# Gated projections and the last up projection with the weights as the stationary operand

## What is computed

```python
def swiglu(h, w_gu, w_down):                       # layers a and b, D_FF = 2816
    gate, up = jnp.split(h @ w_gu, 2, axis=-1)
    return (jax.nn.silu(gate) * up) @ w_down

x = x + swiglu(rmsnorm(x, norm_ffn), w_gu, w_down)            # layers a and b
h = rmsnorm_2(x, norm_mlp[l])                                 # last layer, D_FF_2 = 4096
x = x + jnp.square(jax.nn.relu(h @ w_mlp_in[l])) @ w_mlp_out[l]
```

## Time and profile before

| | us |
|---|---|
| median of 3 runs (lowest, highest) | 972.89 (972.74, 973.11) |
| the profiled execution | 973.31 |
| its span | 971.5 |
| PE busy | 961.4 (99%) |
| LDWEIGHTS busy | 779.4 (80%) |
| DVE busy | 576.1 (59%) |
| ACT busy | 497.2 (51%) |
| DMA | 168.79 MB, mean 174 GB/s |

### The profile page before, as it was taken

One profiled execution on the slowest core, in us unless ns is written; L12 is line 12 of the kernel. 1 busy time (PEld: TensorE's weight loads), 2 busy tenths in 40 slices (PEclk: granted clock), 3 DMA queues, 4 the chain that ended last, 5 costly groups with the idle time before them and its releaser, 6 DMA issues.

```text
span 971.5 us, 12509 instructions
## 1 busy us (share of the span) xinstructions
PE 961.4 (99%) x4848; PEld 779.4 (80%) x4848; DVE 576.1 (59%) x846; ACT 497.2 (51%) x694; POOL 5.7 (1%) x13
## 2 busy tenths in 40 slices
PE   9999999999999999999999999999999999999996
PEld 7878888888888887888888888877777888888885
DVE  6553766655356465765655438588774676546444
ACT  6754544434345674644444337556675454445333
POOL 0000000000000000000000001000000000000000
PEclk9999999999999999999999999999999999999998
DMA  9715555455545420554555549443323455555551
GB/s 359 236 46 189 182 195 191 173 179 200 184 174 204 147 84 31 220 185 175 190 196 194 191 168 346 172 141 113 120 98 131 173 195 183 183 174 195 191 198 44
DMA packets 25926, 168.79 MB, mean 174 GB/s; under 512 B 2792, under 2 KB 3798, under 8 KB 6679
## 3 DMA queue, kind: packets, MB, share of 16 engines
q1 hardware_dynamic: 24412, 163.46, 47.6%
q0 software_dynamic: 1232, 4.57, 1.2%
q10 hardware_dynamic: 235, 0.11, 0.0%
HBM read 167.05 MB, written 1.08 MB: 173 GB/s over the span
## 4 chain that ended last, share of the span: by engine, by line
PE 98%; DVE 1%; ACT 0%; issue 0%; DVEq 0%; ACTq 0%
PE ps L1516 82%; PE ps L1634 2%; PE ps L2198 1%; PE ps L1863 1%; PE ps L2209 1%; PE ps L2310 1%; PE ps L2228 1%; PE ps L1755 1%; PE ps L1933 1%; PE ps L1746 1%; PE ps L1650 1%; PE ps L1592 1%; PE ps L2021 1%; PE ps L1718 0%; PE ps L1795 0%; PE ps L1765 0%
## 5 line engine op out<-in xcount | busy, mean ns | idle before, releaser
L907 DVE TENSOR_TENSOR w_both<-raw,w_both 128x2048 fp32r<-128x2048 f32 x149 | 339.8, 2285 | 187.6 <-ACT w_both L419 187.6
L1516 PE MATMUL ps<-w_both,a_hi 128*128 128x512 f32 (+1 forms) x1504 | 406.3, 392 | 0.6
L419 ACT ACTIVATE w_both<-raw 128x2048 fp32r<-128x2048 f32 x149 | 284.6, 1917 | 172.9 <-DMA raw<-in_down 41.8
L1516 PEld LDWEIGHTS ps<-w_both,a_hi 128*128 128x128 f32 x1504 | 275.4, 188 | 59.4 <-issue 5.9
L1516 PE MATMUL ps<-w_both,a_lo 128*128 128x512 f32 (+1 forms) x752 | 230.1, 387 | 0.0
L1516 PEld LDWEIGHTS ps<-w_both,a_lo 128*128 128x128 f32 x752 | 140.6, 188 | 29.8
L1516 PE MATMUL ps<-w_both,h_hi 128*128 128x512 f32 x576 | 154.8, 391 | 0.0
L1516 PEld LDWEIGHTS ps<-w_both,h_hi 128*128 128x128 f32 x576 | 107.5, 188 | 22.0
L1516 PE MATMUL ps<-w_both,h_lo 128*128 128x512 f32 x288 | 88.6, 389 | 0.0
L1516 PE MATMUL ps<-w_both,m_hi 128*128 128x512 f32 x256 | 71.4, 401 | 0.0
L600 ACT ACTIVATE mlp_a<-ps,tiny 128x256 f32<-128x256 f32 x44 | 18.5, 471 | 100.6 <-PE ps L1516 100.6
(11 more groups left out here) (262 smaller groups left out, 723.2 us busy)
## 6 DMA issues: line engine op xcount, KB each, us to landing
raw<-in_a_gu SPq DMA_DIRECT2D x22, 1024.0 KB, 4.7
raw<-in_b_gu SPq DMA_DIRECT2D x22, 1024.0 KB, 4.7
raw<-in_up SPq DMA_DIRECT2D x16, 1024.0 KB, 4.8
raw<-in_down SPq DMA_DIRECT2D x16, 1024.0 KB, 4.8
raw<-in_a_down SPq DMA_DIRECT2D x11, 1024.0 KB, 4.7
raw<-in_b_down SPq DMA_DIRECT2D x11, 1024.0 KB, 4.7
raw<-in_front SPq DMA_DIRECT2D x8, 1024.0 KB, 4.9
raw<-in_gates SPq DMA_DIRECT2D x8, 1024.0 KB, 4.8
```

Of the source, the lines that this page charges most:

```text
L419: A_(ring(w_hi, us)[:, 0:n], ring(raw, us)[:, 0:n], ACT.Copy).then_inc(s_hi, 1)
L907: V.tensor_tensor(ring(w_lo, us)[:, 0:n], ring(raw, us)[:, 0:n], ring(w_hi, us)[:, 0:n].bitcast(fp32), ALU.subtract).then_inc(s_lo, 1)
L1516: ins = MM(ps[:, b + T, 0:wd], chT(parts[ap_], c, T), wp[wp_][:, off:off + wd], start=(c == first and pn == 0), stop=(c == last and pn == 2))
```

## The change

The three jobs swap the operands. `slices_unit` takes four 128 x 128 blocks of weights of a chunk as stationary operands, one after the other, and moves all 256 tokens past each. A unit becomes 4 x 3 x 4 = 48 matmuls of 256 columns, and the result has the channels on the partitions. The transposes of the results and the argument `between` go. The norm root is now one number for a column: `rms_flips` turns `rst` into a row repeated on all partitions (two transposes a job, in bank 4, called at the third chunk of the job's third unit), and ACT copies it to `rms_rows`. In a_gu and b_gu DVE multiplies gate and up by these rows (two instructions of 512), ACT takes the sigmoid (one of 512), DVE multiplies twice more (512 each), ACT rounds and DVE subtracts, now from SBUF. In up2 DVE does the Relu and the rows in one instruction (1024), ACT squares it twice, once into `mlp_b` and once rounded into `h_hi`, and DVE subtracts.

```diff
-        ("branch_a", 2, 2, "dve"), ("out2", 4, 2, "dve"), ("up2", 16, 8, "act"), ("down2", 16, 2, "dve")]
+        ("branch_a", 2, 2, "dve"), ("out2", 4, 2, "dve"), ("up2", 16, 8, "dve"), ("down2", 16, 2, "dve")]
...
+        rms_rows = kvm[:, 0:S]
...
             pool.wait_ge(s_mm, U0["b_down"] + 1)
+            pool.wait_ge(s_hlo, 22)
             pool.dma_start(gfin[:, :], A["final_norm"].partition_broadcast(P)).then_inc(s_gfin, 16)
...
             pool.wait_ge(s_mm, U0["down2"] + 1)
+            pool.wait_ge(s_hlo, 29)
             pool.dma_start(gfin[:, :], A["norm_final_2"].partition_broadcast(P)).then_inc(s_gfin, 16)
...  ACT, gated
+                        for q in qs:
                             split_hi(U0[name] + 2 * bs + 2 + q, i)
+                        if isinstance(b_of, int) and bs == 0:
+                            rms_rows_copy(n)
+                        act.wait_ge(s_g1, done + b_of + 1)
+                        g0 = 1024 * (bs % 2)
+                        A_(mlp_a[:, g0 + 512:g0 + 1024], mlp_a[:, g0:g0 + 512], ACT.Sigmoid).then_inc(s_sg, 1)
                         if final:
                             split_hi(U0[name] + 2 * bs + 3)
...
+                        act.wait_ge(s_gh, done + b + 1 + 2 * i)
+                        h0 = 1024 * (b % 2)
+                        A_(h_hi[:, bass.ds(512 * b + 1024 * i, 512)], mlp_b[:, h0:h0 + 512], ACT.Copy).then_inc(s_hhi, 1)
...  ACT, up2
+                act.wait_ge(s_gdve, emptied(G0["up2"] - 1, "dve") + b_of + 1)
+                at = 1024 * (bs % 2)
+                A_(mlp_b[:, at:at + 1024], mlp_a[:, at:at + 1024], ACT.Square).then_inc(s_gh, 1)
+                A_(h_hi[:, bass.ds(1024 * bs + 2048 * i, 1024)], mlp_a[:, at:at + 1024], ACT.Square).then_inc(s_hhi, 1)
+            up2(0, 0, (1, 2))
+            up2(1, 0, (1,))
             with act.Fori(0, 2) as i:
                 up2(2, i)
                 up2(3, i)
             up2(6, 0)
-            up2(7, 0, final=True)
-            up2(8, 0, last=True)
+            up2(7, 0, (0,))
+            split_hi(U0["down2"] + 1)
             rest("down2", 16)
...  DVE, gated
+                        dve.wait_ge(s_mm, U0[name] + 2 * bs + 2 + 4 * i)
+                        V.tensor_tensor(halves(g), halves(bank(q)), rows, ALU.mult).then_inc(s_g1, 1)
+                        if not isinstance(b_of, int) or b_of >= 2:
+                            dve.wait_ge(s_hlo, done + b_of - 1)
+                        V.tensor_tensor(halves(h), halves(bank(q + 1)), rows, ALU.mult).then_inc(s_gdve, 1)
                         dve.wait_ge(s_sg, done + b_of + 1)
+                        V.tensor_tensor(g, g, s, ALU.mult).then_inc(s_gm, 1)
                         dve.wait_ge(s_gm, done + b_of + 1)
+                        V.tensor_tensor(h, g, h, ALU.mult).then_inc(s_gh, 1)
                         if final:
                             split_lo(U0[name] + 2 * bs + 3)
...  DVE, up2
+                dve.wait_ge(s_mm, U0["up2"] + 2 * bs + 2 + 4 * i)
+                if not isinstance(b_of, int) or b_of >= 2:
+                    dve.wait_ge(s_hhi, 22 + b_of - 1)
+                V.scalar_tensor_tensor(mlp_a[:, at:at + 1024].rearrange("p (z n) -> p z n", n=S),
+                                       pair_banks(PAIR[G0["up2"] + bs]).rearrange("p b (z n) -> p (b z) n", n=S), 0.0,
+                                       rms_rows.unsqueeze(1).broadcast_to([P, 4, S]), ALU.max, ALU.mult)\
+                    .then_inc(s_gdve, 1)
+                if final:
+                    split_lo(U0["up2"] + 2 * bs + 3)
+                dve.wait_ge(s_gh, 22 + b_of + 1)
+                dve.wait_ge(s_hhi, 22 + b_of + 1)
...  TensorE
+            def slices_unit(us, i, q, g, before=None, need=None):
+                pe.wait_ge(s_lo, us + 1 + 4 * i)
+                for k in range(4):
+                    c = 4 * q + k
...
+                    for pn, (ap_, wp_) in enumerate(PASSES):
+                        for s in range(4):
+                            at = 512 * k + P * s
+                            ins = MM(bank(2 * PAIR[g] + s // 2, S * (s % 2), S * (s % 2) + S),
+                                     ring((w_hi, w_lo)[wp_], us)[:, at:at + P], ch(AH[ap_], c),
...
+            def rms_flips(norm):
+                def call():
+                    pe.wait_ge(s_rst, NORM[norm] + 1)
+                    for T in range(2):
+                        ins = nc.tensor.transpose(bank(4, P * T, P * T + P), rst[norm][:, T:T + 1].broadcast_to([P, P]),
+                                                  ident[:, :])
+                    ins.then_inc(s_rT, 1)
...
-                    flip(1, i)
                     mult(3, i)
-                    flip(2, i)
...
-            wide_job("a_down", 11, HH, need=hidden(0), between=a_last_flip, tail=x_flips("a_down", 0))
+            wide_job("a_down", 11, HH, need=hidden(0), tail=x_flips("a_down", 0))
...
-            wide_job("down2", 16, HH, need=lambda c: pe.wait_ge(s_hlo, 22 + c // 4 + 1),
-                     between=lambda: up_flip(7, 0), by_tile=True)
+            wide_job("down2", 16, HH, need=lambda c: pe.wait_ge(s_hlo, 22 + c // 4 + 1), by_tile=True)
```

More of the change, by code:

```diff
@@ L584, in _, with rms_rows_copy, gated_act, body @@
             rest("a_out", 4)
-            def gated_act(name, done, norm):
-                def body(bs, i, last=False, final=False, entry=False):
+            def rms_rows_copy(n):
+                act.wait_ge(s_rT, n)
+                A_(rms_rows, bank(4, 0, S), ACT.Copy).then_inc(s_rb, 1)
+            def gated_act(name, done, n):
+                def body(bs, i, qs=(0, 1), last=False, final=False):
                     b_of = bs + 2 * i
                     if not last:
-                        for q in range(1 if entry else 0, 1 if final else 2):
+                        for q in qs:
                             split_hi(U0[name] + 2 * bs + 2 + q, i)
[L593 to L602, removed]
+                        if isinstance(b_of, int) and bs == 0:
[3 more added lines that the diff above has]
+                        A_(mlp_a[:, g0 + 512:g0 + 1024], mlp_a[:, g0:g0 + 512], ACT.Sigmoid).then_inc(s_sg, 1)
                         if final:
@@ L619, in _ @@
             act.preload_act_table(ACT.Sigmoid)
-            gated_act("a_gu", 0, "a_ffn")
+            gated_act("a_gu", 0, 1)
             for j in range(2, 10):
@@ L835, in _, with up2 @@
             enter_norm("mlp2", "out2", "mlp2", [(GCOL["norm_mlp_2"], a_hi)], "up2")
-            def up2(bs, i, last=False, final=False, entry=False):
+            def up2(bs, i, qs=(0, 1)):
                 b_of = bs + 2 * i
[L839 to L861, removed]
+                for q in qs:
+                    split_hi(U0["up2"] + 2 * bs + 2 + q, i)
+                if isinstance(b_of, int) and bs == 0:
+                    rms_rows_copy(3)
+                act.wait_ge(s_gdve, emptied(G0["up2"] - 1, "dve") + b_of + 1)
[4 more added lines that the diff above has]
+            up2(1, 0, (1,))
             with act.Fori(0, 2) as i:
@@ L1079, in _, with gated_dve, halves, body @@
             rest("a_out", 4)
-            def gated_dve(name, done, norm):
-                def body(bs, i, last=False, final=False, entry=False):
+            def gated_dve(name, done, n):
+                def halves(t):
+                    return t.rearrange("p (z n) -> p z n", n=S)
+                rows = rms_rows.unsqueeze(1).broadcast_to([P, 2, S])
+                def body(bs, i, qs=(0, 1), last=False, final=False):
                     b_of = bs + 2 * i
                     if not last:
-                        for q in range(1 if entry else 0, 1 if final else 2):
+                        for q in qs:
@@ L1098, in body @@
-                        times(g, 0, s_gm)
+                        q = 2 * PAIR[G0[name] + bs]
+                        g, s, h = (t[:, 1024 * (bs % 2) + o:1024 * (bs % 2) + o + 512]
+                                   for t, o in ((mlp_a, 0), (mlp_a, 512), (mlp_b, 0)))
+                        if isinstance(b_of, int) and bs == 0:
+                            dve.wait_ge(s_rb, n)
+                        dve.wait_ge(s_mm, U0[name] + 2 * bs + 2 + 4 * i)
+                        V.tensor_tensor(halves(g), halves(bank(q)), rows, ALU.mult).then_inc(s_g1, 1)
@@ L1120, in _ @@
             dve.wait_ge(s_tabd, 16)
-            gated_dve("a_gu", 0, "a_ffn")
+            gated_dve("a_gu", 0, 1)
             rest("a_down", 11)
@@ L1407, in _, with up2 @@
             enter_norm("mlp2", "out2", 4, "mlp2", [(GCOL["norm_mlp_2"], a_hi, a_lo)], "up2")
-            def up2(bs, i, last=False, final=False, entry=False):
+            def up2(bs, i, qs=(0, 1), final=False):
                 b_of = bs + 2 * i
[L1411 to L1427, removed]
@@ L1428, in _ @@
-            up2(0, 0, entry=True)
-            up2(1, 0)
+                for q in qs:
+                    split_lo(U0["up2"] + 2 * bs + 2 + q, i)
+                at = 1024 * (bs % 2)
```

(11 more changed lines are left out.)

103 lines of the change are left out of this document (39 added, 64 removed).

## The result

| | before | changed |
|---|---|---|
| median of 5 runs (lowest, highest), us | 973.04 (972.74, 973.21) | 979.70 (977.64, 980.85) |
| ratio, 95% interval | | 1.0066 [1.0054, 1.0078] |
| profiled execution, its span | 973.31, 971.5 | 979.66, 977.9 |

The changed kernel is 6.7 us slower; 3.7 had been forecast. The spread of its runs is new as well: 3.2 us against 0.5.

The account below looks back on a forecast made before the run. TensorE's own instruction order was taken as the bound. Transposes -17.9, swapped matmuls +17.8, norm rows +0.8, waits +2.3 in down2 and +0.7 in a_down and b_down gave +3.7 us, a median of 976.6, range 973 to 982.

Parts of the forecast that it names:

- Transposes: In a_gu, b_gu and up2: removing 22 gated groups at 0.484 us and 8 up2 groups at 0.912 saves 17.9 us.
- The price of the swapped form: In the three swapped jobs: 1440 added loads at 12.4 ns, with 119.5 ns a 256-column matmul, cost 17.8 us.
- the prediction's own sign: In the gated and up2 loops: a group period off 11.47 us would show the matmul price wrong.
- a fixed 12 to 13 ns with the load hidden: 256-column matmuls on TensorE: streaming plus this fixed part sets the pace, the load hidden with 9 ns to spare.
- the 66-column row: Profile row of 16 matmuls with a 66-column block and 256 moving columns, 118.8 ns each, taken as the low end.
- Break-even: In the swapped jobs: 118.2 ns a matmul would make the changed kernel no slower.
- rival (b): In the loops: the load becomes the pace at 121 to 123 ns, total time 981 to 987 us; chance 0.13.
- Rival (a): Not slower: 118.8 ns a matmul in the loops and shorter down-job waits, 972.5 us with 2 us less waiting; chance 0.14.
- Norm rows: Two row transposes in each of the three swapped jobs, with a margin, cost 0.8 us together.
- Emptying covered: In the swapped jobs' loops: emptying a group costs nothing, covered by the 11.5 us of the next group.
- Waits at the down jobs: TensorE waits for the split at the second unit: 2.3 us in down2, 0.36 each in a_down and b_down.
- What follows a wait: Behind the down-job waits: no further cost was priced, down2's wait counting only its 2.3 us.

Follow-up runs that it names:

- the gated jobs alone: Gated jobs of a and b swapped as in the changed kernel, up2 and the head of down2 as before the change; 977.73 us, ratio 1.0047.
- up2 alone: Against the kernel before: only up2 swapped, with down2's second unit split before the last up2 group; 971.15 us, ratio 0.9978.
- the 64-column blocks: Changed kernel with all down-job second units split early, stationary blocks in the swapped jobs cut from 128 to 64 columns, half the weights left out; 956.62 us.
- the longer wait: Changed kernel with two extra unused 512-element squares on ACT ahead of the split of down2's second unit; 981.09 us, ratio 1.0072.

## Why the forecast was right in sign and short in size

Direction and cause hold: the transposes removed and the loads added nearly cancel, and the new waits at the down jobs decide. The steps in their order:

- **Transposes, -17.9 us.** Right. The run with the gated jobs alone and the one with up2 alone both come out with 0.484 and 0.912 us a group (4.5 measured for 4.4, -2.0 for -2.0).
- **The price of the swapped form, +17.8.** This term was mis-sized: 120.0 ns and not 119.5, 19.2 us and not 17.8. By the prediction's own sign a period off 11.47 us would show this price to be wrong, and the period is 11.52. The mean over 21 distances from 960.70 on includes a first one of 113 ns that belongs to the change of shape; from the second group of the kernel before,

```profile
961.05 0.40 PE L1592 MATMUL ps<-w_both,h_hi 128*128 128x256 f32 x2
```

  to the last there are 18 in 2.16 us, 120.0 each. Half a nanosecond, 2880 times, is 1.4 us. The reason given beside it, a fixed 12 to 13 ns with the load hidden, fell to the 64-column blocks (113.4 ns): the 66-column row, read there as proof that the width doesn't matter, is no proof of it two columns below. The number was good only because the row had exactly the shape in question; the neighbours of another shape, 118.8 and 110, would not have given it.
- **Break-even and rival (b).** The paces that (b) feared, 121 to 123 ns in the busy middle, didn't come: 120.0 there as at the quiet end. Rival (a) needed 118.2.
- **Norm rows, +0.8.** 0.22 us a job, 0.66.
- **Emptying covered.** Right: 936 and 648 matmuls in one block each, without a wait.
- **Waits at the down jobs, 2.3 and 2 x 0.36.** Right in place, cause and nearly in size: 2.2 and 0.28 twice. Taking them away gave more than they last: 0.84 for the two short ones.
- **What follows a wait, 0.** This step was missing. The prediction priced 2.3 us of waiting at 2.3 us. In the profiled execution TensorE ran at 1.2 GHz behind it and lost 1.7 more (some 0.2 of it the slow start that full clock shows too), and the runs with and without the wait (979.1 and 975.9) differ by 3.2. The kernel before has no wait within down2 to read this from, but the steps of the prediction said that a full stop of TensorE would appear, and the granted clock should have been asked about then.

3.7 + 1.4 + 1.7, less 0.4 for the terms that came out smaller, is 6.4, the difference of the two spans; the medians differ by 6.7. The sum leaves out the slow starts behind the two short waits (2 x 0.18) and the 0.18 by which the changed kernel was ahead at the end of a_out, which go against each other.

## What to carry to other kernels

Which operand stands still is a trade of loads against transposes, and the break-even is an arithmetic one: here 48 added loads (0.64 us) against four transposes (0.48, a loss) or eight (0.91, a gain), so that swapping one of three jobs beats swapping all. Read the price of a matmul from a row of exactly its shape, leave out the first distance after a change of shape, and multiply by the count before rounding. When a change makes a saturated TensorE stop for about 2 us, look for the work queued ahead of what it waits for and move it; the stop cost more than its length at 0.28 us (0.4) and at 1.2 us (1.4), and far more where the clock fell behind it (3.9 for 2.2).

## What the runs showed of the hardware that was not expected

- Behind a pause of 2.0 us in an otherwise unbroken stream the granted clock fell to 1.2 GHz in both executions of the changed kernel that were profiled, and behind one of 3.1 us in the longer wait's; 512-column matmuls took 426 ns each instead of 226.7, and 1.7 us were lost in the two of the changed kernel. The fall came with the first matmul behind the pause in one, after three and after six of them in the others. A pause of 1.1 us (one profile) was followed by no fall, nor was one of 2.5 us in the kernel with 64-column blocks and 192 tokens. So a fall is possible behind 2 us, and not certain.
- A pause has a price at full clock as well: the first 12 matmuls of 512 columns behind the waits at a_down take 2.90 us instead of 2.72.
- Distance between matmuls that each bring a load, by block columns and moving columns: 120.0 ns (128, 256), 118.8 (66, 256), 113.4 (64, 256), 111.6 (128, 192), 88.7 (64, 192), and 113.4 or 117.8 (32, 256). 256 more moving columns cost 226.7 - 120.0 = 106.7 ns, so even where a matmul streams for 107 ns a part of its price goes with the width of the block, and a narrower block isn't always cheaper.
